# Sixteen table scatters behind expert 1's gather, five early list entries, and weight loads in 16 KB runs, in a hybrid block with 32 experts

## The reference

```python
u2 = rms_norm(h, norm_ffn_g[l])
h = h + moe_ffn(u2.reshape(-1, d), router_w[l], router_b[l], expert_w1[l], expert_b1[l],
                expert_w2[l], expert_b2[l]).reshape(h.shape)
...
logits = xt.astype(jnp.float32) @ router_w.astype(jnp.float32) + router_b.astype(jnp.float32)
top_val, top_idx = lax.top_k(logits, TOP_K)
gates = jax.nn.softmax(top_val, axis=-1).astype(xt.dtype)
...
hcat = xb @ w1[e] + b1[e]
h_glu, h_lin = jnp.split(hcat, 2, axis=-1)
h_glu = jnp.minimum(h_glu, SWIGLU_LIMIT)
h_lin = jnp.clip(h_lin, -SWIGLU_LIMIT, SWIGLU_LIMIT)
act = h_glu * jax.nn.sigmoid(SWIGLU_ALPHA * h_glu) * (h_lin + 1.0)
return act @ w2[e] + b2[e]
...
return jnp.einsum('nk,nkd->nd', gates, ys[dest])
```

## Time and profile before

| | |
|---|---|
| median of 3 runs | 1573.57 us (1573.24 to 1574.15) |
| profiled execution, its own time | 1575.7 us |
| its span, first to last instruction | 1573.9 us |
| PE busy | 1535.8 us (98%) |
| DMA traffic | 492.26 MB, mean 313 GB/s over the span |
| granted PE clock, mean | 0.992 |

### The profile page before, as it was taken

One profiled execution on the slowest core, in us unless ns is written; L12 is line 12 of the kernel. 1 busy time (PEld: TensorE's weight loads), 2 busy tenths in 40 slices (PEclk: granted clock), 3 DMA queues, 4 the chain that ended last, 5 costly groups with the idle time before them and its releaser, 6 DMA issues.

```text
span 1573.9 us, 38127 instructions
## 1 busy us (share of the span) xinstructions
PE 1535.8 (98%) x15984; PEld 862.4 (55%) x15984; DVE 743.8 (47%) x1563; ACT 282.7 (18%) x406; POOL 523.7 (33%) x677
## 2 busy tenths in 40 slices
PE   7999999999999998999999999999999999999996
PEld 6998988877889633433343334334333433343344
DVE  4799899015233633533443344335334433443367
ACT  5333133356222300100010010001000100100001
POOL 7333433463334553222222322222222223222224
PEclk9999999999999999999999999999999999999998
DMA  7553243221275399999999999999999999999994
GB/s 221 161 171 124 60 144 119 81 81 54 80 295 219 119 366 414 384 419 419 417 419 419 418 419 419 419 418 419 419 419 417 419 420 419 419 420 419 418 419 206
DMA packets 131700, 492.26 MB, mean 313 GB/s; under 512 B 16405, under 2 KB 74153, under 8 KB 81988
## 3 DMA queue, kind: packets, MB, share of 16 engines
q1 hardware_dynamic: 111892, 463.30, 74.2%
q0 software_dynamic: 10128, 17.25, 3.0%
q10 hardware_dynamic: 9632, 11.03, 2.2%
HBM read 475.46 MB, written 24.87 MB: 318 GB/s over the span
## 4 chain that ended last, share of the span: by engine, by line
PE 85%; DMA 6%; POOL 3%; DVE 1%; issue 1%; ACT 1%; SPq 1%; POOLq 0%; DVEq 0%; ACTq 0%
PE banks L1603 36%; PE banks L1140 28%; PE banks L1632 19%; DMA w_ring<-in_expert_w_dram 4%; DMA stage<-in_w_in_dram 1%; DMA code_of<-slot_table 1%; SPq L462 0%; POOL slot_table L722 0%; DMA slot_table<-code,dest 0%; DMA xs<-u_rows,piece_now 0%; PE banks L1499 0%; POOL h_res L794 0%; POOL xs L704 0%; PE banks L1372 0%; POOL w_lo L627 0%
## 5 line engine op out<-in xcount | busy, mean ns | idle before, releaser
L1603 PE MATMUL banks<-w_ring,xT 128*32 128x512 f32 x6144 | 668.2, 594 | 6.2 <-DVE xT L2108 5.3
L1603 PEld LDWEIGHTS banks<-w_ring,xT 128*32 128x32 f32 x6144 | 193.1, 110 | 461.7 <-issue 456.4
L1632 PE MATMUL banks<-w_ring,actT 128*32 128x256 f32 x6144 | 338.1, 379 | 0.4 <-DMA w_ring<-in_expert_w_dram 0.3
L2086 DVE TENSOR_TENSOR hid<-banks,bias_now 128x512 f32<-128x512 f32 x96 | 63.9, 665 | 470.7 <-PE banks L1603 470.7
L1632 PEld LDWEIGHTS banks<-w_ring,actT 128*32 128x32 f32 x6144 | 192.7, 110 | 153.7 <-issue 19.3
L636 POOL TENSOR_TENSOR w_lo<-stage,w_hi 128x2048 fp32r<-128x2048 f32 x38 | 175.3, 4612 | 258.1 <-ACT w_hi L847 258.1
L695 POOL TENSOR_TENSOR carrier<-carrier 1x1 f32<-1x1 f32 x161 | 30.8, 192 | 576.7 <-DVE y_out L2117 423.7
L1114 ACT ACTIVATE sig<-hid 128x256 f32<-128x256 f32 x96 | 40.0, 417 | 909.4 <-DVE hid L2087 909.4
L1140 PE MATMUL banks<-u_hi,w_hi 128*128 128x264 f32 (+1 forms) x528 | 176.7, 335 | 0.9 <-POOL w_lo L627 0.9
L1140 PE MATMUL banks<-u_hi,w_lo 128*128 128x264 f32 (+1 forms) x528 | 175.0, 331 | 0.0
L1140 PE MATMUL banks<-u_lo,w_hi 128*128 128x264 f32 (+1 forms) x528 | 174.7, 331 | 0.0
(11 more groups left out here) (306 smaller groups left out, 1472.9 us busy)
## 6 DMA issues: line engine op xcount, KB each, us to landing
w_ring<-in_expert_w_dram SPq DMA_DIRECT2D x384, 1024.0 KB, 15.7
stage<-in_w_in_dram SPq DMA_DIRECT2D x20, 1024.0 KB, 5.2
stage<-in_w_in_dram SPq DMA_DIRECT2D x16, 512.0 KB, 5.8
y_rows<-empty_row ACTq DMA_DIRECT2D x8, 1024.0 KB, 4.9
y_in<-y_rows SPq DMA_DIRECT2D x4, 2048.0 KB, 24.2
stage<-in_conv_pw_w_dram SPq DMA_DIRECT2D x4, 1024.0 KB, 5.1
stage<-in_mlstm_out_w_dram SPq DMA_DIRECT2D x4, 1024.0 KB, 5.1
stage<-in_w_out_dram SPq DMA_DIRECT2D x4, 1024.0 KB, 5.3
```

The lines of the kernel that those rows point to most:

```text
L1603: last = nc.tensor.matmul(banks[32 * g:32 * (g + 1), t].rearrange("p (c j) -> p c j", j=64), xT[:, t, k], units, start=k == 0, stop=k == K ...
L1632: last = nc.tensor.matmul(banks[32 * g:32 * (g + 1), 3 + t, 0:GRP], actT[:, t, k], w2_ring[k // 2][:, k % 2, GRP * g:GRP * (g + 1)], start ...
L2086: own(nc.vector.tensor_tensor(hid[:, t], banks[:, t], bias1, ALU.add))
```

## The change

Four things are changed together.

- All 16 table scatters are issued after expert 1's gather; before, eight of them preceded it.
- From the table that is read back, POOL first makes only the first `EARLY` entries for all t in one set of five instructions. (The diff adds `EARLY = 4` at the top of the file, but the function has its own `EARLY = 5`, which is the one that counts, as the shapes 128x3x5 below show.) With these it writes expert 0's results and gathers expert 2's rows; the full lists, `last_g` and the loop come after that.
- The ring has six pieces of 2 MB instead of twelve of 1 MB: four of `w1`, two of `w2`. A partition gets one run of 16 KB for each. A piece is asked for when both of its k blocks (or all four of `w2`) have been used. New semaphores `row_turn` keep the pace of the gathers as it was.
- The layout that follows from it: `normed_rows` needs eight instructions instead of four for each tile and reads every second element; biases, router weights and the activation's product use other strides.

```diff
-RING = 12
-W1C = KT
+RING = 6
+W1C = KT // 2
...
-RC = DFF * 2
+RC = DFF * 4
...
             def load_chunk(e, c):
 
                 if c < W1C:
-                    src = expert_w1[0, bass.ds(e, 1), P * c:P * (c + 1), :].rearrange("e p (g n) -> p (e g) n", g=2)
+                    src = expert_w1[0, bass.ds(e, 1), 2 * P * c:2 * P * (c + 1), :].rearrange("e (p k) n -> p (e k) n", p=P)
                     sp.dma_start(w1_ring[c], src).then_inc(ring_in[c], 16)
                 else:
                     m = c - W1C
-                    src = expert_w2[0, bass.ds(e, 1), 2 * P * m:2 * P * (m + 1), :].rearrange("e (p k) n -> p (e k) n", p=P)
+                    src = expert_w2[0, bass.ds(e, 1), 4 * P * m:4 * P * (m + 1), :].rearrange("e (p k) n -> p (e k) n", p=P)
                     sp.dma_start(w2_ring[m], src).then_inc(ring_in[c], 16)
...
             pool.wait_ge(table_set, 16)
-            for i in range(2):
-                places_out(i)
-
             for i in range(TT):
                 pool.wait_ge(u2_stored[i], 16)
             pool.wait_ge(tables_made, CG * TG)
             pool.sem_inc(idx_step, 1)
             request_rows()
-            for i in range(2, TT):
+            for i in range(TT):
                 places_out(i)
...
+            lists_of(code_of[:, 0:TG, 0:EARLY], token_part[:, 0:TG, 0:EARLY], piece_of[:, :, 0:EARLY], row_of[:, :, 0:EARLY])
+            nc.gpsimd.tensor_copy(row_now, row_of[:, :, 0]).then_inc(idx_step, 1)
+            pool.wait_ge(idx_step, 3 + TG)
+            pool.wait_ge(y_emptied, 16 * KT)
+            results_out(0, 1)
+            pool.wait_ge(xT_made, 2 * TG)
+            gather(2, 8 + TG, 2)
             for t in range(TG):
-                codes = code_of[:, t::TG]
...
+                lists_of(code_of[:, t::TG], token_part, piece_of[:, t, 0:PASSES * NE].rearrange("p (q e) -> p q e", e=NE),
+                         row_of[:, t, 0:PASSES * NE].rearrange("p (q e) -> p q e", e=NE))
...
                     for k in range(KT - LATE):
-                        pe.wait_ge(ring_in[k], (n + 1) * 16)
+                        if k % 2 == 0:
+                            pe.wait_ge(ring_in[k // 2], (n + 1) * 16)
                         for t in range(TG):
                             last = hidden(k, t)
-                        last.then_inc(ring_used[k], 1)
-
-                    for k in range(KT - LATE, KT):
-                        pe.wait_ge(ring_in[k], (n + 1) * 16)
+                        last.then_inc(ring_used[k // 2] if k % 2 else row_turn[k // 2], 1)
+
+                    pe.wait_ge(ring_in[W1C - 1], (n + 1) * 16)
...
                 for g in range(CG):
-                    nc.vector.scalar_tensor_tensor(out=u2[:, i, GRP * g:GRP * (g + 1)].rearrange("p (k j) -> p k j", j=32),
-                                                   in0=of_group(h_res[:, i], g), scalar=h_rstd[:, i:i + 1], in1=of_group(gf_bc, g),
-                                                   op0=ALU.mult, op1=ALU.mult).then_inc(u2_made, 1)
+                    for b in range(2):
+                        nc.vector.scalar_tensor_tensor(out=u2[:, i, GRP * g:GRP * (g + 1)].rearrange("p (m b j) -> p b m j", b=2, j=32)[:, b],
+                                                       in0=of_group(h_res[:, i], g)[:, b], scalar=h_rstd[:, i:i + 1],
+                                                       in1=of_group(gf_bc, g)[:, b], op0=ALU.mult, op1=ALU.mult).then_inc(u2_made, 1)
```

More of the change, by code:

```diff
@@ L44 @@
 EPS = 1e-5
+EARLY = 4
 NE = 32
@@ L204, in hybrid_block @@
         chunk = size([P, RC])
-        w1_ring = [at(f"w1_ring{c}", [P, 2, DFF], F32, ring_end - chunk * (c + 1)) for c in range(W1C)]
-        w2_ring = [at(f"w2_ring{c}", [P, 2, D], F32, ring_end - chunk * (W1C + c + 1)) for c in range(RING - W1C)]
+        w1_ring = [at(f"w1_ring{c}", [P, 2, 2 * DFF], F32, ring_end - chunk * (c + 1)) for c in range(W1C)]
+        w2_ring = [at(f"w2_ring{c}", [P, 4, D], F32, ring_end - chunk * (W1C + c + 1)) for c in range(RING - W1C)]
         assert ring_end - chunk * RING >= gates_at + chan
@@ L372, in hybrid_block @@
         xs_in, xT_made, idx_step = sem("xs_in"), sem("xT_made"), sem("idx_step")
+        row_turn = [sem(f"row_turn{t}") for t in range(TG)]
         in_slot_made, rows_mm = sem("in_slot_made"), sem("rows_mm")
@@ L494, in _ @@
             sp.dma_start(h_res, x[0].rearrange("(i p) d -> p i d", p=P)).then_inc(row_bc_in, 16)
-            for c in range(4):
+            for c in range(2):
                 load_chunk(0, c)
@@ L499, in _ @@
             sp.wait_ge(mm_done, pair_tick(PW_PAIR + 1, 8))
-            for c in range(4, 6):
-                load_chunk(0, c)
+            load_chunk(0, 2)
             load_pair(WO_PAIR + 1, lambda s: w_source(WO_PAIR, s, 1))
@@ L505, in _ @@
             sp.wait_ge(mixed, KT)
-            for c in range(6, RING):
+            for c in range(3, RING):
                 load_chunk(0, c)
@@ L548, in load_results @@
                     if i < TT - 1:
-                        for c in range(2 * (TT - 2 - i), 2 * (TT - 2 - i) + 2):
-                            sp.wait_ge(ring_used[c], n + 1)
+                        sp.wait_ge(ring_used[TT - 2 - i], n + 1)
                     sp.dma_start(y_in[i], results[i].rearrange("p (k d) -> p k d", k=TOPK)).then_inc(y_loaded[i], 16)
@@ L740, in _, with lists_of @@
             pool.wait_ge(rows_in, 16 * CG)
-            for t in range(TG):
-                codes = code_of[:, t::TG]
[L743 to L749, removed]
+            def lists_of(codes, tokens, pieces, rows):
+                chain(nc.gpsimd.tensor_scalar(tokens, codes, -1.5, 0.25, ALU.add, ALU.mult))
+                chain(nc.gpsimd.tensor_scalar(tokens, tokens, TO_WHOLE, None, ALU.add))
+                chain(nc.gpsimd.tensor_scalar(tokens, tokens, -TO_WHOLE, None, ALU.add))
+                nc.gpsimd.tensor_scalar(pieces, tokens, float(CG), group_of, ALU.mult, ALU.add)
+                chain(nc.gpsimd.tensor_scalar(rows, codes, float(CG), group_of, ALU.mult, ALU.add))
@@ new lines, in results_out @@
+            def results_out(n, stored):
+                for t in range(TG):
+                    pool.wait_ge(y_made, n * TG + (t + 2))
+                    carry_wait(1 + t)
+                    pool.indirect_dma_start(out=y_dram, out_offset=bass.IndirectOffsetOnAxis(ap=row_now[:, t:t + 1], axis=0),
+                                            in_=y_out[:, t], in_offset=None, bounds_check=last_row,
+                                            oob_is_err=False).then_inc(y_stored, 16)
+                pool.wait_ge(y_stored, stored * (16 * TG))
+                carry_wait(1 + TG)
@@ L805, in of_group @@
         def of_group(rows, g):
-            return rows.rearrange("p (k g j) -> p g k j", g=CG, j=32)[:, g]
+            return rows.rearrange("p (m g j b) -> p g b m j", g=CG, j=32, b=2)[:, g]
         def rows_copied(i, f):
@@ L1601, in hidden @@
                         for g in range(CG):
[L1602 to L1603 removed]
+                            units = w1_ring[k // 2][:, k % 2].rearrange("p (c g j) -> p g c j", g=CG, j=128)[:, g]
+                            last = nc.tensor.matmul(banks[32 * g:32 * (g + 1), t].rearrange("p (c j) -> p c j", j=128),
                                                     xT[:, t, k], units,
@@ L1620, in expert @@
                             last = hidden(k, t)
-                            if t == TG - 1 and k < KT - 1:
-                                last.then_inc(ring_used[k], 1)
+                            if t == TG - 1 and k == KT - LATE:
+                                last.then_inc(ring_used[k // 2], 1)
                         last.then_inc(hid_mm, 1)
```

45 lines of the change are left out of this document (19 added, 26 removed).

## The result

The changed kernel takes 1583.2 us (median, 1581.5 to 1584.5, 5 runs) against 1573.57 (1572.95 to 1574.15, 5 runs): a ratio of 1.0059, interval 1.0048 to 1.0070. It is slower by 9.6 us; 1580 was forecast. The profiled execution has a span of 1582.7 us, 8.8 above that of before, and its own time is 1584.47.

A forecast was written before the change was run, and what follows sets the result against it. The prediction took PE, busy 98% of the span, as the bound. Expert 2's later start +8.3, late weights -2.2 and layout +0.55 gave +6.6 us on 1573.57, rounded to 1580; range 1571 to 1585.

The forecast's parts named there:

- the rival (small transfers wait out 16 KB packets): The forecast itself: small transfers wait out 16 KB packets, PE idles 10 to 16 us ahead of expert 2; chance 0.56.
- five of six links: POOL's chain to expert 2's start: last scatter +10.2, landing +0.6, `code_of` +3.6, lists -9.0, results +1.5, gather +2.0 less 0.6.
- the cure of the late weights: At the last experts, a better DMA rate from 16 KB runs removes PE's 2.2 us of waiting for weights.
- the rate of 423: Weights' DMA in 700 to 1300 us: 16 KB runs were expected to give 423 GB/s or more, against 419.
- The `code_of` term: Reading the table back: 190 small packets over 16 engines, 12 each, wait 0.30 us longer apiece, +3.6 us.
- the last table scatter, 2 packets, +0.6: Landing of the last table scatter before the table's reading: its 2 packets wait out longer weight packets, +0.6 us.
- The layout (+0.55): Eight instructions of 128 elements per tile instead of four of 256; the last tile's delay the first expert, +0.55 us.
- The clock's price ahead of expert 2: PE's matmuls after the idle ahead of expert 2 lose to the lower granted clock, again 2.7 us as now.
- Rival 3: Faster: later scatters could meet a gap in the weights' queue, PE doesn't idle, 1563.9 us; chance 0.14.
- Rival 2: Small transfers go as before: 1572.4 us, or 1574.6 without the rate gain; chance 0.24.
- Rival 4: Slower still: PE waits for 2 MB pieces repeatedly, 0.4 us an expert over the last 20, 1585 to 1590; chance 0.06.
- The eight ahead were hidden: Eight scatters ahead of expert 1's gather ran almost wholly within POOL's wait for DVE; moving them behind costs +10.2 us.

The follow-up runs named there:

- e4b: Changed kernel with each 2 MB piece loaded as two DMAs with 8 KB runs, repeated on another chip: 1579.90 us, ratio 1.0029.
- e9: Changed kernel with all sixteen table scatters ahead of expert 1's gather and 8 KB runs: 1571.51 us, ratio 0.9980.
- e1b: Kernel before with only the scatters moved, all sixteen behind expert 1's gather, repeated on another chip: 1584.36 us, ratio 1.0057.
- e5: Kernel before with 16 KB runs and their layout alone, eight scatters ahead, full lists: 1580.66 us, ratio 1.0037.
- e3: Changed kernel with eight table scatters ahead of expert 1's gather and eight behind, as before: 1570.79 us, ratio 0.9940.
- e6: Changed kernel, 16 KB runs kept, with all sixteen table scatters ahead of expert 1's gather: 1563.65 us, ratio 0.9938.
- e8: Changed kernel with expert 1's third piece and those behind it asked for only after the table is read: 1570.23 us, ratio 0.9982.
- e1: Kernel before with only the scatters moved, all sixteen behind expert 1's gather, first chip: 1584.08 us, ratio 1.0033.
- r_after: Changed kernel, unedited, measured and profiled again: 1582.85 us, ratio 1.0063 against the kernel before.
- r_before: Kernel before, unedited, measured and profiled again: 1574.49 us, ratio 1.0009.
- e4: Changed kernel with each 2 MB piece loaded as two DMAs with 8 KB runs, first chip: 1583.79 us, ratio 1.0020.
- e2: Kernel before with the early lists alone, eight scatters ahead and 8 KB runs: 1577.01 us, ratio 0.9989.

## Why the prediction was right or wrong

**Right**: the side, the rival (small transfers wait out 16 KB packets), five of six links within 0.3 us, the place (idle ahead of expert 2), the cure of the late weights (-2.05 of -2.2; e4b, e9 and e1b with 8 KB have them, e5, e3 and e6 with 16 KB don't) and the rate of 423.

**The `code_of` term** (+3.6, measured +3.86) came from a count of packets in the earlier trace rows and the length of a packet. After, while `code_of` lands (588 to 592 us), the two queues still alternate:

```profile
q1 hardware_dynamic: 85, 1.15, 91.6%
q0 software_dynamic: 85, 0.14, 12.2%
```

The Trainium skill, page DMA: Bandwidth & Descriptors, section Queues, rings and completion order, has an engine go round its queues packet by packet; these counts agree. The preference for packets of at most 4096 B in the section SWDGE vs HWDGE vs iDMA stands there among what GpSimd builds. It is no bound on the weights' packets, which SP issues: 1.15 MB in 85 packets is 13.5 KB each, and the reading is 3 to 5 us longer for it in five 16 KB runs.

**The step that failed is "the last table scatter, 2 packets, +0.6"**, measured +5.95. The step counted the packets of the last scatter alone and not those queued ahead of them. Read like the `code_of` stretch, the trace of before has 129 small packets to go at that point, 8 for each engine; at the forecast's 0.30 us each that would have been +2.4. After, 217 were to go, and 17 weights packets passed each engine at 0.69 us (15 at 0.37 before). With 8 KB packets (e1b, e4b) the landing is 7.4 to 8.5 us, with eight scatters behind 16 KB ones 6.3 (e5). So the miss, +5.3 us, is an interaction of the two edits, and neither alone has it. Its mechanism is shown only in part, as e5 doesn't fit the price by turns. Added alone, the scatters' move costs a ratio of 1.0057 and the 16 KB runs 1.0037.

**Three small terms were off the other way.** The layout (+0.55) measured 0: POOL had `piece_now` at 544.23 instead of 544.38. A tile's eight instructions take 2.19 us, near the 2.25 forecast, but DVE's wait of 0.72 us ahead of the last tile is gone, and from the third tile's start to the logits it needs 4.36 us instead of 4.24. The forecast let that wait cover the third tile only. The clock's price ahead of expert 2, 22.21 - 20.78 = 1.43 us instead of 2.71. And the tail, which was forecast at nothing: from expert 31's last matmul to the end it is 2.3 us shorter, 0.60 of it a wait for DVE that is gone, 1.3 in two groups of matmuls that run in part at the low clock, and 0.4 behind PE's last matmul. Windows of the tail's first matmuls, of before and then of after:

```profile
1543.00:1550.00 7.00, 4.58 (x48) 3.41 (x48) 6.96 (x9) 0.00 (x0) 1.49 (x3) 0.70 0.75 311
1550.00:1556.00 6.00, 6.00 (x41) 4.43 (x38) 3.80 (x5) 2.34 (x5) 0.77 (x2) 0.78 0.15 66
```

```profile
1553.00:1560.00 7.00, 4.86 (x64) 3.37 (x56) 6.96 (x10) 0.00 (x0) 4.88 (x6) 0.83 0.15 56
1560.00:1566.00 6.00, 6.00 (x45) 4.53 (x42) 5.08 (x5) 3.09 (x5) 1.48 (x3) 0.91 0.00 0
```

A granted clock between the levels of 1.2 and 2.4 GHz means a part of the window at either. Why less of it is at 1.2 after wasn't tried; in e1b, e3 and e9 the two groups take 4.0 us together, against 6.9 before and 5.6 after, so it doesn't go with the length of the runs. The sum: +14.42 - 1.28 - 2.05 - 2.3 = +8.8 us, the span's difference. The forecast had 8.3 + 0.55 - 2.2 = 6.6. The 6.1 us too little on the chain were hidden to two thirds by 4.1 too many in clock, tail and layout: the total was nearer than its parts.

**Rival 3**, that later scatters might meet a gap in the weights, described the landing in e8 and e1 and not the changed kernel: where a gap exists the landing is 2.9 us, but nothing in the change makes one. **Rival 2** falls with e5 and `code_of`. **Rival 4**: no late weights.

**"The eight ahead were hidden"** holds from both sides: moving them back costs 10 to 12 us (e1b: last scatter at 568.86 for 558.18, expert 2 at 620.31 for 608.50), and moving the other eight ahead as well (e6) costs nothing at the gather. The prediction saw that expert 1's gather gains nothing by leading; the lesson it didn't draw is that the gather had over 10 us to spare.

## What to carry to other kernels

Price a row of small transfers beside a busy queue by what is still queued when the last one is issued, not by the last one alone: here 13.6 packets for each engine stood there instead of 2. Count in the same stretch how many of the other queue's packets pass, and how long one takes. Two edits that each leave a wait alone can lengthen it together, so a sum of single prices needs a term for the pair, or a run with both. Send what a later chain waits for before the big transfers start, and let what has slack go behind it: the same edits in another order take 1563.65 us against 1582.85 on one chip. Longer runs pay where transfers are the bound (8 KB to 16 KB with sixteen ahead: ratios of 0.9980 and 0.9938) and cost where a chain of small transfers is.

## What the runs showed of the hardware

**Small writes slow the weights themselves.** While sixteen scatters of 4 B elements land, the engines are as busy as ever and move half. Windows of 556 to 576 us, of the changed kernel and then of e4b:

```profile
556.00:576.00 20.00, 20.00 (x287) 12.67 (x283) 12.32 (x30) 2.53 (x4) 10.55 (x11) 1.00 0.99 236
```

```profile
556.00:576.00 20.00, 20.00 (x288) 9.54 (x284) 12.36 (x30) 2.53 (x4) 10.84 (x12) 1.00 0.96 216
```

236 and 216 GB/s at a share of 0.99 and 0.96, where 423 and 419 are had later; the small packets themselves take under 3%. The same page of the Trainium skill, DMA: Bandwidth & Descriptors, section Specifications, says that transfers under 512 B become a read-modify-write; the trace agrees that they cost far more than their bytes, but not by which mechanism. In the same window the rate is 245 (r_after) and 227 (e1b) with sixteen scatters behind the gather, 314 and 310 with eight (before, r_before), 277 with eight and 16 KB (e5), and 333 and 328 with none (e6, e9). That the scatters are the cause is read from this order, not from a run that leaves them out. With the lower rate a weights packet takes 0.69 us in the landing and not the 0.61 of the forecast.

**One chip held PE up inside expert 0**, in all four kernels run on it and in none of eight on two others: 13.6 us with sixteen scatters behind the gather (e1, e4), 5 with eight (e2, e3), as gaps put down to issue. The third of the 16 KB packets on the instruction queue (q8) in this stretch came in 582 to 585 us there (e1, e4) and in 571 to 573 in the two traces that the result is read from. Whether late code held PE up, or a late PE asked for its code late, isn't shown. The kernel before had a median of 1579.11 on that chip, 4.6 and 6.5 us above the other chips, so it probably was held up too. Without e1b and e4b the corner of 16 scatters at 8 KB would have been read wrongly, as 2.4 and 4.6 us.

**A longer idle of PE was followed by less loss to the low clock**: idles of 5.26, 7.00 and 8.04 us by matmuls of 23.49, 23.58 and 23.43 us, idles of 15.09, 17.02, 19.51 and 20.25 by 22.31, 22.95, 22.21 and 22.62, where 20.78 is the full clock. The mean granted clock of these stretches is 0.88, 0.88 and 0.89 after the shorter idles, 0.93, 0.90, 0.93 and 0.92 after the longer ones. No run was made for it.
